# A two-layer decoder trunk: a query block moved behind the first expert units, a second front five units later, token means in short waits, a first weight block in three pieces

## The reference, cut to what matters

```python
q = (xi @ wq).reshape(Tb, PEER_HEADS, 2, PEER_DQ // 2)
s = jnp.einsum('thcd,hcnd->thcn', q, subkeys)
s1, i1 = lax.top_k(s[:, :, 0], K)
s2, i2 = lax.top_k(s[:, :, 1], K)
...
top_s, pos = lax.top_k(cand, K)
eidx = jnp.take_along_axis(cidx, pos, axis=-1)
g = jax.nn.softmax(top_s, axis=-1)
act = gelu(jnp.einsum('td,thkd->thk', xi, u[eidx]))
out = jnp.einsum('thk,thkd->td', g * act, v[eidx])
```

## Time and profile before

| | |
|---|---|
| median of 3 runs | 1676.3 us (1675.14 to 1677.28) |
| the profiled execution | 1675.74 us, its span 1673.9 us |
| PE busy, share of the span | 1337.2 us, 80% |
| DVE, ACT, POOL busy | 59%, 46%, 37% |
| bytes moved | 667.98 MB, mean 399 GB/s |
| of these the gathers (q0), the weights (q1) | 536.90 MB, 129.52 MB |
| chain that ended last | DMA 39%, PE 32%, DVE 11%, ACT 8% |
| mean granted TensorE clock | 0.86 |

### The profile page before, as it was taken

The page is one execution under the profiler, slowest core; times in us unless marked ns, Lnnn a source line. Parts: engine busy times, 40 slices in busy tenths (PEclk is TensorE's granted clock), DMA queues, the critical chain, the costliest instruction groups (busy, mean ns, idle before and its releaser), DMA issues.

```text
span 1673.9 us, 24232 instructions
## 1 busy us (share of the span) xinstructions
PE 1337.2 (80%) x8622; PEld 686.3 (41%) x8622; DVE 995.4 (59%) x2534; ACT 770.0 (46%) x1996; POOL 624.0 (37%) x516
## 2 busy tenths in 40 slices
PE   9999999796885988888697568878799556667776
PEld 7788755362550425344364125345255111111110
DVE  1455766964558845664545985574447975545554
ACT  2332458555434644564543454573544443343333
POOL 0001232443333442343333443333333445556663
PEclk9999999997996998998799689999789786676666
DMA  9537999999999999999999999999999999999997
GB/s 376 228 109 298 369 423 404 421 420 421 422 424 420 419 423 423 417 421 424 419 422 423 419 418 422 417 412 424 419 423 420 418 420 421 420 421 422 420 421 296
DMA packets 87338, 667.98 MB, mean 399 GB/s; under 512 B 9632, under 2 KB 12080, under 8 KB 14128
## 3 DMA queue, kind: packets, MB, share of 16 engines
q0 software_dynamic: 73728, 536.90, 77.4%
q1 hardware_dynamic: 13488, 129.52, 18.9%
HBM read 665.33 MB, written 1.05 MB: 398 GB/s over the span
## 4 chain that ended last, share of the span: by engine, by line
DMA 39%; PE 32%; DVE 11%; ACT 8%; issue 6%; POOL 3%; SPq 0%; POOLq 0%; DVEq 0%; PEldq 0%; ACTq 0%
DMA arena<-in_experts,idxT 38%; PE psum L617 32%; DVE arena L1771 6%; POOL arena L2199 3%; ACT L1174 2%; ACT cst L1174 1%; ACT ring L1174 1%; ACT gelus L1174 1%; ACT gains L1174 1%; DMA ring<-in_ev_sk 1%; ACT sqb L1174 1%; ACT L1179 1%; DVE rstd L1662 0%; DVE red L1739 0%; DVE rstd L1650 0%
## 5 line engine op out<-in xcount | busy, mean ns | idle before, releaser
L2199 POOL DMA_INDIRECT arena<-in_experts,idxT x512 | 623.8, 1218 | 1027.6 <-PE psum L617 782.9
L617 PE MATMUL psum<-arena,cst 64*64 64x512 f32 (+1 forms) x4102 | 686.9, 756 | 309.2 <-ACT cst L1174 303.9
L1771 DVE CUSTOM_DVE_ANT_0 arena<-arena,xrow 128x1024 f32<-128x1024 f32 x512 | 622.2, 1222 | 498.4 <-DMA arena<-in_experts,idxT 489.8
L1174 ACT ACTIVATE gelus<-red,small 128x1 f32<-128x1 f32 x512 | 150.1, 293 | 681.5 <-DVE red L1771 664.0
L617 PEld LDWEIGHTS psum<-arena,cst 64*64 64x64 f32 (+1 forms) x4102 | 128.9, 153 | 705.5 <-ACT cst L1174 625.7
L617 PEld LDWEIGHTS psum<-hT,ring 128*128 128x128 f32 x2304 | 275.5, 196 | 102.4 <-issue 95.1
L617 PE MATMUL psum<-hT,ring 128*128 128x128 f32 x2304 | 298.4, 285 | 6.4 <-DMA ring<-in_ev_sq 2.1
L1174 ACT ACTIVATE cst<-cst,gains 128x128 f32<-128x128 f32 x512 | 206.3, 403 | 21.6 <-PE psum L617 4.9
L1174 ACT ACTIVATE gains<-gelus,gateT 128x1 f32<-128x1 f32 x512 | 150.9, 295 | 16.8
L1174 ACT ACT_TABLE_LOAD x66 | 84.7, 1283 | 1.2
L617 PEld LDWEIGHTS psum<-mixT,ring 128*128 128x128 f32 (+1 forms) x592 | 70.5, 194 | 27.3 <-issue 24.0
(11 more groups left out here) (237 smaller groups left out, 895.3 us busy)
## 6 DMA issues: line engine op xcount, KB each, us to landing
ring<-in_pq SPq DMA_DIRECT2D x15, 2048.0 KB, 7.7
ring<-in_ev_out SPq DMA_DIRECT2D x4, 2048.0 KB
ring<-in_xq SPq DMA_DIRECT2D x4, 2048.0 KB
ring<-in_xo SPq DMA_DIRECT2D x4, 2048.0 KB
arena<-in_experts,idxT POOLq DMA_INDIRECT x512
ring<-in_od_out SPq DMA_DIRECT2D x4, 2048.0 KB
ring<-in_ev_sk SPq DMA_DIRECT2D x2, 2048.0 KB
ring<-in_ev_sv SPq DMA_DIRECT2D x2, 2048.0 KB, 17.9
```

Source lines behind the costliest of these rows:

```text
L617: return nc.tensor.matmul(out, lhsT, rhs, start=start, stop=stop)
L1174: return nc.scalar.activation(out, in_, f, **k)
L1771: V.tensor_tensor_reduce(out=ut, in0=ut, in1=xrow[:, u // PAIRS, :], scale=1.0, scalar=0.0, op0=ALU.mult, op1=ALU.add, accum_out=dots[:, k ...
L2199: nc.gpsimd.indirect_dma_start(slot[slot_of(u)], None, d["experts"], bass.IndirectOffsetOnAxis(ap=idxT[:, u:u + 1], axis=0))\
```

## The change

Five edits go together. The last query block of the first half, `pq00.3`, its scores `ps00.3` and the scores `ps00.2` leave the opening stretch: `LAST_QUERIES = 106` puts them at tail clock 106 instead of 92, which is units 2 to 7. The second half's first front starts at 1 instead of -4, five units later. `mean_ev.1` goes from clock -12 into `tail(0, 0)`, in three pieces (2, 3 and 3 products) ahead of waits of the cross-attention; its squares go to `sqb`, behind the root for `mean_xa00`. The block `ev_sq0` is loaded in pieces of 0.5, 0.5 and 1 MB. `ps00.0` goes ahead of `xr00.1`. The banks of PSUM are dealt out anew for the jobs concerned.

```diff
-FIRST_FROM = (-108, -4)
-NORM_AHEAD = (0, 9)
+FIRST_FROM = (-108, 1)
+LAST_QUERIES = 106
...
-        jobs[-1:] = [(81, f"xr{e}.0"), (81, f"xr{e}.1"), (81, f"ps{e}.0"), (81, f"mean_ffn{e}")]
+        jobs[-1:] = [(81, f"xr{e}.0"), (81, f"ps{e}.0"), (81, f"xr{e}.1"), (81, f"mean_ffn{e}")]
...
-    jobs += [(92, f"pq{e}.3"), (93, f"ps{e}.2"), (97, f"ps{e}.3")]
+    last = 92 if l or t else LAST_QUERIES
+    jobs += [(last, f"pq{e}.3"), (last + 1, f"ps{e}.2"), (last + 5, f"ps{e}.3")]
...
                 if b == 0:
-                    sp.dma_start(dst[:, 0], src[:, 0]).then_inc(half_loaded, 16)
-                    sp.dma_start(dst[:, 1], src[:, 1]).then_inc(w_loaded[s], 16)
+                    sp.dma_start(dst[:, 0], src[:, 0]).then_inc(quarter_loaded[0], 16)
+                    sp.dma_start(dst[:, 1], src[:, 1]).then_inc(quarter_loaded[1], 16)
+                    sp.dma_start(dst[:, 2:4], src[:, 2:4]).then_inc(w_loaded[s], 16)
...
-                    if t == j == 0:
-                        pe.wait_ge(half_loaded, 16)
+                    if t == 0 and j < 2:
+                        pe.wait_ge(quarter_loaded[j], 16)
...
                 yield from until(g + 61)
+                next_means = halves_of_means("ev", 0, 1, (1, 4)) if q == 0 else iter(())
+                next(next_means, None)
                 pe.wait_ge(xq_sq, q + 1)
...
                 yield from until(g + 70)
+                next(next_means, None)
                 copied(pe, f"xt{e}.0", f"xt{e}.1")
...
                 yield from until(g + 72)
+                next(next_means, None)
                 copied(pe, f"xm{e}")
...
                             flip_rows(0)
+                            key_scores(0, of=range(2))
                             flip_rows(1)
-                            key_scores(0, of=range(2))
                             token_means()
...
-                    yield from features4(f"pq{e}.{n}", f"pq{e}{n}", 512, 0, hh, KC, beats(80 + 4 * n),
+                    yield from features4(f"pq{e}.{n}", f"pq{e}{n}", 512, 0, hh, KC,
+                                         beats(LAST_QUERIES if q == 0 and n == 3 else 80 + 4 * n),
...
-                yield from until(g + 97)
+                yield from until(g + (97 if q else LAST_QUERIES + 5))
                 key_scores(3)
...
                 root("xa", f"mean_xa{e}")
+                if q == 0:
+                    squares("ev", 0, 1, 0)
+                    squares("ev", 0, 1, 1)
...
                 copy_out(f"xm{e}", oh)
+                if q == 0:
+                    copied(act, f"xq{e}")
+                    root("ev", "mean_ev.1")
...
                 for n in range(4):
-                    yield from until(g + 84 + 4 * n)
+                    last = LAST_QUERIES - 92 if q == 0 else 0
+                    yield from until(g + 84 + 4 * n + (last if n == 3 else 0))
...
-                    yield from until(g + 86 + 4 * n)
+                    yield from until(g + 86 + 4 * n + (last if n >= 2 else 0))
...
                 g = FIRST_FROM[t]
-                yield from until(g + 6)
+                yield from until(g + (5 if t else 6))
```

More of the change, by code:

```diff
@@ L235, in first_jobs @@
         slots += [(24, 3, "norm_mem"), (28, 3, "xk0.0"), (30, 3, "xk0.1"), (36, 3, "xkn0.0"), (36, 3, "xkn0.1"), (42, 3, "xv0.0")]
-        slots += [(FIRST_FROM[n] - NORM_AHEAD[n] + 1 - FIRST_FROM[0], 5 * n, f"mean_ev.{n}") for n in range(TT)]
+        slots.append((1, 0, "mean_ev.0"))
     slots += [(s + TAIL_LAG[t], 4, n) for s, n in tail_jobs(0, t)]
@@ L271, in psum_jobs @@
         put([n for n in names if n.startswith("zr")], accumulators[3:4])
-        put([n for n in names if n[:2] not in ("zs", "zr")], front + accumulators[:2] if t == 0 else front)
+        names = [n for n in names if n[:2] not in ("zs", "zr")]
+        last = ("pq00.3", "ps00.2", "ps00.3")
+        put([n for n in names if n not in last], front + accumulators[:2] if t == 0 else front)
+        put([n for n in names if n in last], front)
         if t == 0:
             put(["xv0.1"], accumulators[3:4])
+            put(["mean_ev.1"], accumulators[2:3])
     for l in range(LAYERS):
@@ L433, in trunk @@
         in_gate, in_const = sem("in_gate"), sem("in_const")
-        cleared, half_loaded = sem("cleared"), sem("half_loaded")
+        cleared, quarter_loaded = sem("cleared"), [sem(f"quarter_loaded{n}") for n in range(2)]
         in_rest, in_mem = sem("in_rest"), sem("in_mem")
@@ L1152, in _ @@
                 for t in range(TT):
-                    experts(l, t, ahead, previous)
+                    experts(l, t, first + ahead, previous)
                     previous = (l, t)
@@ L1271, in mixer @@
                 g, plan = FIRST_FROM[t], PLAN[t]
-                yield from until(g - NORM_AHEAD[t])
                 if t == 0:
+                    yield from until(g)
                     load_table(EXP_LN_SET)
                     act.wait_ge(in_x, 16)
-                squares("ev", 0, t, 0)
-                squares("ev", 0, t, 1)
-                yield from until(g - NORM_AHEAD[t] + 2)
-                root("ev", f"mean_ev.{t}")
+                    squares("ev", 0, t, 0)
+                    squares("ev", 0, t, 1)
+                    yield from until(g + 2)
+                    root("ev", f"mean_ev.{t}")
                 yield from until(g + plan["sk"] + plan["a_unit"] % 2)
@@ L1575, in _ @@
                 for t in range(TT):
-                    experts(l, t, ahead, closed)
+                    experts(l, t, first + ahead, closed)
                     closed.append((l, t))
```

18 lines of the change are left out of this document (9 added, 9 removed).

## The result

The changed kernel is slower: median 1680.15 us (1677.98 to 1683.67, 8 runs) against 1675.13 (1674.93 to 1677.82, 8 runs, those shown ahead among them), ratio 1.0030, interval 1.0020 to 1.0039. I had forecast 1671.4, and slower with a chance of 0.08. That forecast stood on a median of 1676.3 from three runs; over all eight the kernel before is 1.2 us lower. As a change I forecast -4.9 us, and +5.0 was measured. The profiled execution took 1683.18 us, at the upper end of its spread, and the first thing to learn is why.

The account below looks back on a forecast made before the run. DMA engines were taken as the bound from about 160 us on. Terms -3.25 - 1.71 + 0.1 - 0.2 + 0 = -5.1, rounded to -4.9, gave 1670.8 profiled and 1671.4 median, range 1669.3 to 1675.6.

Parts of the forecast that it names:

- First hole, -3.25: DMA at 147 GB/s from 189 to 194 us; closes with the query block behind units 0 and 1, saving 3.25 us.
- the low rate behind the hole: DMA at 368 GB/s from 194 to 206 us, 1.51 us lost; left as it is, ends -1.5 and +1.5.
- The front five units later: Step on the load of out010: five more gathers issued ahead of it close the hole at 270 to 278, -1.71 us.
- Closes with 4.1 us to spare: At out010: DMA has 5.8 us more in hand where it lacked 1.71, so the hole there closes, -1.71.
- The second hole: DMA at 331 GB/s from 270 to 278 us, PE fully busy, shortly before out010's load; 1.71 us lost.
- rival (a): From 206 us to out010 PE is the bound and the hole only moves: gain 1.7, time 1674.6; chance 0.19.
- Rival (d): PE's clock stays at 1.2 GHz in short pieces after its wait, making gathers late: slower, 1681.5 us; chance 0.08.
- Its second cause: DVE's crowded stretch at 500 to 560 us, 52.41 of 60 busy, slides five units towards the next layer's front; unpriced.
- Means +0.1: Opening stretch: mean products in pieces of 2, 3 and 3 ahead of short waits cost 0 to +0.3, taken as +0.1.
- `ps00.0` -0.2: Opening stretch: scores moved past 4 transposes bring the first gather earlier, -0.2 us, between -0.5 and 0.
- three pieces 0: Start: ev_sq0 in three loads; what sq.0 gains is waited for at sk.0, 0 us, between 0 and +0.4.

Follow-up runs that it names:

- e2_halves: The changed kernel with its first block loaded in two pieces of 1 MB again; 1680.62 us, ratio 1.0031 to the kernel before.
- e6_early_routes: The kernel before with routing steps of heads 4 to 7 and their gates five units earlier, front unmoved; 1680.96 us, ratio 1.0029.
- e3_routes: The changed kernel with routing steps of heads 4 to 7 and their gates five units later too; 1674.84 us, ratio 0.9993.
- e4_both: e2_halves with routing steps of heads 4 to 7 and their gates five units later too; 1673.58 us, ratio 0.9988.
- e12_front_alone: e2_halves with the last query block back before unit 0 (LAST_QUERIES = 92), routing unmoved; 1680.15 us, ratio 1.0023.
- e7_queries_early: e4_both with the last query block back before unit 0 (LAST_QUERIES = 92); 1673.16 us, ratio 0.9983.
- e5_nomove: e2_halves with front and query block moved back, leaving the means and the order of ps00.0; 1676.40 us, ratio 0.9994.
- e1_pieces: The kernel before with only ev_sq0 loaded in three pieces instead of two; 1676.15 us, ratio 1.0005.
- e11_spread: e7_queries_early with heads 6 and 7 routed at units 60 and 62 instead of 53 and 55; 1673.70 us, ratio 0.9985.
- e13_half_gv: e4_both with half of gv.1's matmuls on PE left out; 1673.74 us, ratio 0.9985.

## Why the prediction was wrong

- **First hole, -3.25**: right in its mechanism, and it closed. In e2_halves 160 to 200 gives -4.3; the low rate behind the hole, which I had left as it was, went with it. What failed is that the gain lasts: with the block put back, no time is lost (below).
- **The step that failed** is "The front five units later". I followed what the shift does to the DMA engines at one place, `out010`, and put everything else that moves or stays at nothing, without a reason. Of the moved front every step on DVE counts, and the steps of routing that do not move with it stand in its way. That costs +5.8 (e2_halves), shown by e6_early_routes, which makes it without the move, and by e3_routes and e4_both, which take it away (5.3 and 7.0 us in the medians). The sign stood in the trace of before: DVE's last scores at 317.48 and `ranks` at 322.72, five us apart, where the front was to move five units of three us and more.
- **"Closes with 4.1 us to spare"**, the term -1.71 of the same step, was wrong too. The second hole went only from its old place: in e2_halves 200 to 280 gives -1.3, and 280 to 300 costs +3.0. e12_front_alone shows some 2 us of it moving with the front alone. What the two holes were to give was given back on the way: rival (a), to which I had given 0.19. e7_queries_early and e12_front_alone show it in the time for the query block alone: -3.25 in my sum, nothing that can be told when it is put back. My price for (a), a gain of 1.7, is near the -1.8 of e4_both, which has (a) and no pile. That is partly luck: e7_queries_early gains as much (-2.4) without the query block's part, from which I had worked the price out.
- **The whole miss** is 9.9 us, from -4.9 to +5.0. The pile is 5.3 to 7.0 of it. With 7.0, what is left is 2.9, close to the 3.1 us between the forecast and the -1.8 of e4_both.
- **Rival (d)** ended on the right side (1681.5 for 1680.15) and by another road: the clock was 1.00 in 189 to 270, where I feared it low, and fell later, behind DVE's waits. So that its price came near is luck. Its second cause named the right kind of collision at the wrong place: 500 to 560 lost nothing (422 GB/s).
- **Means +0.1, `ps00.0` -0.2, three pieces 0**: too small for these runs to tell right from wrong (e5_nomove, e1_pieces). I had not thought of a late start such as that of the profiled execution.

The best that came out is e7_queries_early, 1673.16: the second half's front and the routing of heads 4 to 7 five units later, the query block where it was. It is 0.17% under the kernel before (interval 0.03 to 0.31%), less than the 0.2% I called measurable, and it is the lowest of all that were tried. Its neighbours e4_both and e11_spread are 0.12 and 0.15% under.

## What to carry to other kernels

When a block of work is shifted along a schedule, list for every engine what the block's steps will stand beside in its new place, above all work pinned to fixed positions by another table; move both, or neither. A hole that closes in a stretch where the engines hand work round in a circle is worth something only once the same trace shows no later place that sets the pace; try the edit alone before adding its gain to a sum. Before reading a single profiled execution against another, compare where their first common event stands: here 2.8 of 7.4 us between the two profiles were such a chance.

## What the runs showed of the hardware

PE's granted clock fell to about half behind some waits of about two to four us between long stretches of work (1.88 us, then 0.52; 2.00, then 0.50; 3.02, then 0.50; 3.63, then 0.67 and 0.50), and did not after 1.99 us in e1_pieces. The fall costs some 1.6 us in `sk.0` (9.04 for 7.41) and lasts some 10 us in e13_half_gv. Why one wait of two us brings it and another does not stays open. Of 16 profiled executions, of as many kernels, two started late (first gathers at 164.10 and 164.46, the others 160.2 to 162.1); what decides when `ev_sk0` lands was not found.
